# Normalising x four tiles at a time and moving the preparation of the unit conditions behind block 0's convolution

## The reference

```
shift, scale, gate = jnp.split(sc @ mod_w[i] + mod_b[i], 3, axis=-1)
cshift, cscale, cgate = jnp.split(scc @ mod_w[i] + mod_b[i], 3, axis=-1)
h_lat = rms_norm(x, norm_g[i]) * (1.0 + scale[:, None]) + shift[:, None]
h_ctx = rms_norm(ctx, norm_g[i]) * (1.0 + cscale) + cshift
...
u_lat, g_lat = jnp.split(h_lat @ w_in, 2, axis=-1)
u_ctx, g_ctx = jnp.split(h_ctx @ w_in, 2, axis=-1)
xc_lat = dwconv(u_lat, conv_w, conv_b)
xc_ctx = dwconv(u_ctx, conv_w, conv_b)
```

## Time and profile before

| | |
|---|---|
| median of 3 runs | 2920.01 us (2918.03 to 2926.49) |
| the profiled execution | 2916.92 us, of which the span is 2915.2 us |
| PE busy | 2729.0 us, 94% of the span |
| DVE busy | 1832.3 us, 63% |
| ACT busy | 1212.9 us, 42% |
| DMA, mean over the span | 168 GB/s |

### The profile page before, as it was taken

One profiled execution on the slowest core, in us unless ns is written; L12 is line 12 of the kernel. 1 busy time (PEld: TensorE's weight loads), 2 busy tenths in 40 slices (PEclk: granted clock), 3 DMA queues, 4 the chain that ended last, 5 costly groups with the idle time before them and its releaser, 6 DMA issues.

```text
span 2915.2 us, 41872 instructions
## 1 busy us (share of the span) xinstructions
PE 2729.0 (94%) x14546; PEld 2196.1 (75%) x14546; DVE 1832.3 (63%) x2708; ACT 1212.9 (42%) x1859; POOL 314.7 (11%) x437
## 2 busy tenths in 40 slices
PE   5799999889899999999999899999998998999989
PEld 2477777678677777777778677888886776998879
DVE  4499999889646555465655522334545787774654
ACT  3256555522443434443444422323444224553643
POOL 1101001144000000000003100000000442110000
PEclk8799999999999999999999999999999997999999
DMA  8755545467355454454535454232221663883425
GB/s 361 293 169 184 163 158 169 144 218 232 145 180 195 160 187 173 173 182 179 186 116 185 150 190 148 93 99 88 73 72 44 208 207 123 285 279 110 129 91 168
DMA packets 118632, 488.90 MB, mean 168 GB/s; under 512 B 13584, under 2 KB 15632, under 8 KB 103440
## 3 DMA queue, kind: packets, MB, share of 16 engines
q1 hardware_dynamic: 74176, 267.49, 27.2%
q0 software_dynamic: 44368, 220.22, 21.9%
HBM read 485.56 MB, written 2.10 MB: 167 GB/s over the span
## 4 chain that ended last, share of the span: by engine, by line
PE 66%; DVE 18%; issue 8%; DMA 5%; ACT 2%; DVEq 1%; POOL 0%; ACTq 0%; POOLq 0%; SPq 0%
PE psum L247 17%; PE psum L249 17%; PE psum L248 17%; DVE w_lo L229 4%; DVE psum L334 4%; PE psum L261 3%; DMA y<-in_mod_weights 2%; DVE work L336 2%; DMA work<-in_mod_units 1%; PE psum L1459 1%; PE psum L935 1%; PE psum L978 1%; DVE work L820 1%; ACT w_hi L221 1%; PE psum L284 1%
## 5 line engine op out<-in xcount | busy, mean ns | idle before, releaser
L247 PE MATMUL psum<-h_hi,w_hi 128*128 128x512 f32 (+1 forms) x3808 | 1358.3, 357 | 60.0 <-DVE h_lo L461 34.0
L249 PE MATMUL psum<-h_hi,w_lo 128*128 128x512 f32 (+1 forms) x3808 | 1320.7, 347 | 0.0
L248 PE MATMUL psum<-h_lo,w_hi 128*128 128x512 f32 (+1 forms) x3808 | 1320.5, 347 | 0.0
L229 DVE TENSOR_TENSOR w_lo<-raw,w_hi 128x1024 fp32r<-128x1024 f32 x496 | 597.5, 1246 | 617.2 <-ACT w_hi L221 617.1
L247 PEld LDWEIGHTS psum<-h_hi,w_hi 128*128 128x128 f32 x3808 | 727.7, 191 | 181.0 <-DVE w_lo L229 38.5
L248 PEld LDWEIGHTS psum<-h_lo,w_hi 128*128 128x128 f32 x3808 | 729.1, 191 | 93.7 <-issue 10.0
L249 PEld LDWEIGHTS psum<-h_hi,w_lo 128*128 128x128 f32 x3808 | 727.9, 191 | 89.5
L221 ACT ACTIVATE w_hi<-raw 128x1024 fp32r<-128x1024 f32 x496 | 496.7, 1051 | 291.1 <-PE psum L249 276.7
L334 DVE SCALAR_TENSOR_TENSOR psum<-work,modraw 128x1024 f32<-128x1024 f32 x128 | 177.6, 1388 | 19.4 <-DMA work<-in_mod_units 19.2
L336 DVE SCALAR_TENSOR_TENSOR work<-work,modraw 128x1024 f32<-128x1024 f32 x128 | 162.1, 1266 | 0.0
L267 POOL DMA_DIRECT2D modraw<-in_mod_weights x80 | 42.6, 533 | 836.5 <-PE psum L261 826.9
(11 more groups left out here) (260 smaller groups left out, 2683.6 us busy)
## 6 DMA issues: line engine op xcount, KB each, us to landing
raw<-in_weights SPq DMA_DIRECT2D x496, 512.0 KB, 4.5
modraw<-in_mod_weights POOLq DMA_DIRECT2D x96, 1024.0 KB, 5.2
work<-in_mod_units POOLq DMA_DIRECT2D x128, 512.0 KB, 4.3
y<-in_mod_weights POOLq DMA_DIRECT2D x16, 1024.0 KB, 9.4
modraw<-in_mod_units POOLq DMA_DIRECT2D x32, 512.0 KB, 4.6
modraw<-in_cond_rows POOLq DMA_DIRECT2D x4, 1024.0 KB, 6.3
work<-in_gate_w POOLq DMA_DIRECT2D x16, 256.0 KB, 5.0
work<-in_x_t POOLq DMA_DIRECT2D x16, 256.0 KB, 3.6
```

What stands on the lines that cost most here:

```text
L229: dve.tensor_tensor(w_lo[:, par, half, :], raw[:, 2 * par + half, :], w_hi[:, par, half, :].bitcast(F32), ALU.subtract).then_inc(S["split_ ...
L247: pe.matmul(dst, hi, h_hi[:, k, 0:n], start=(k == 0), stop=False)
L248: pe.matmul(dst, hi, h_lo[:, k, 0:n], start=False, stop=False)
L249: mm = pe.matmul(dst, lo, h_hi[:, k, 0:n], start=False, stop=(k == KT - 1))
```

## The change

Four edits, and one that follows from them:

- The multiplication by the reciprocal root goes from two instructions over 16 tiles ahead of everything into `modulate(j)`, two instructions over four tiles each time. `mod_add(1)` thereby stands directly behind the reciprocal root on DVE.
- On ACT `mod_rows(1)` goes ahead of the four `split_hi` of the first two strips.
- On PE `mod_turn(1)` goes ahead of `products(2)`.
- `cb_tanh(0)` goes into block 0 on ACT, behind the high part of the next u strip; `cb_silu(0)` goes into block 0 on DVE, behind the convolution and the low part of the next u strip.
- ACT no longer waits for `h_ready` ahead of `cb_tanh(0)`; POOL's program is the same, and its wait for `cond_ready` 5 ahead of unit 0's loads remains.

```
@@ lru_act, block
                 next_strip(split_hi, act, su)
+                if isinstance(b, int) and b == 0:
+                    cb_tanh(act, 0)
                 act.wait_ge(S["strip_done"], sg.s + 1)
...
-            act.wait_ge(S["h_ready"], KT)
-            cb_tanh(act, 0)
             block(0, 0)
@@ lru_dve
             dve.wait_ge(S["pads_zero"], 1)
-            cb_silu(dve, 0)
...
                 next_strip(split_lo, dve, su)
+                if isinstance(b, int) and b == 0:
+                    cb_silu(dve, 0)
                 unit(dve, 2 * b, 0, GATE + b)
@@ start_act
             norm_sqrt(act, 0)
+            mod_rows(act, 1, first_bank[1])
             for c in range(2):
                 split_hi(act, 0, c)
...
-            mod_rows(act, 1, first_bank[1])
             high(0)
@@ start_dve
             dve.wait_ge(S["rstd_done"], 1)
-            for x, s in ((xl[:, :, :], 0), (y[:, 1, :, :], 1)):
-                dve.tensor_tensor(x, x, nb["rstd"][:, s * T:(s + 1) * T].unsqueeze(1).to_broadcast([P, KT, T]),
-                                  ALU.mult).then_inc(S["xn_done"], 1)
...
                 ks = bass.ds(4 * j, 4)
+                for s, x in enumerate((xl[:, ks, :], y[:, 1, ks, :])):
+                    dve.tensor_tensor(x, x, nb["rstd"][:, s * T:(s + 1) * T].unsqueeze(1).to_broadcast([P, 4, T]),
+                                      ALU.mult).then_inc(S["xn_done"], 1)
                 dve.wait_ge(S["mod_cols"], 2 * j + 2)
...
-                dve.wait_ge(S["xn_done"], 2)
+                dve.wait_ge(S["xn_done"], 2 * j + 2)
@@ start_pe
             norm_pe(pe, 0)
+            mod_turn(pe, 1, 0, first_bank[1])
             for j in range(1, MOD_FIRST // 2):
                 for par in range(2):
                     products(2 * j + par, par)
-                    mod_turn(pe, 2 * j + par - 1, 0, first_bank[1 - par])
+                    if j > 1 or par > 0:
+                        mod_turn(pe, 2 * j + par - 1, 0, first_bank[1 - par])
```

## The result

The changed kernel took 2928.94 us in the median of 7 runs (2926.09 to 2936.66), the kernel before 2918.93 us beside it (2909.28 to 2926.49). The ratio is 1.0044 with a 95% interval of 1.0026 to 1.0061, so 8 to 18 us slower. In a second series on another occasion the ratio was 1.0036 (1.0023 to 1.0049), in medians 2929.03 to 2917.00. The forecast was 2931 with a range of 2923 to 2937, from a sum of 12.1 us over the kernel before; the medians give 10.0 and 12.0, the ratios 12.8 and 10.5.

The account below looks back on a forecast made before the run. The prediction took transfers, with one hole, to bound the start and DVE to set the pace in the LRU blocks. Its terms, 2.5 us (start) + 9.6 us (block 0) = 12.1 us on a base of 2919, gave 2931 us, range 2923 to 2937.

Parts of the forecast that it names:

- The start bound by transfers: Start, from 18 us on: chunks of modulation weights set the pace, with one hole in the transfers around 50 to 56 us.
- the stall of 3.55 us: Start: PE stands until 61.76 us for DVE's mod_add(1); removing it was put at no gain, upper end 3.55 us.
- The turn ahead of the products delays the refill by 2.5 us: Start: group 3's first load issued 1.3 + 1.6 - 0.4 = 2.5 us later, carried whole to the start's end.
- The multiplication by parts is covered: Start, modulate on DVE: 2.35 us more per group; idle time covers groups 1 and 2, PE's margin group 3.
- the 0.8 us that I counted: End of start: tile 12 ready at 130.2 us, PE wanting it at 131.0; 0.8 us of cover.
- Block 0 costs 9.6 us: LRU block 0, DVE: silu 5.1 us plus 4.5 us standing still for unit 0's load, 9.6 in sum.
- DVE carries it to the end: LRU blocks to output stage: DVE has no idle time to swallow 9.6 us, so output starts later by all of it.
- DVE's delay is swallowed: Rival, LRU blocks: PE sets the pace, DVE has over 9.6 us to spare; only 2.5 us left, 2921.5; chance 0.08.
- PE's stall was real: Rival, start: the wait delayed the slots' refill, so 3.55 us come back; 6.1 us slower, 2925; chance 0.14.
- DVE's early work was the bound: Rival, start: it followed DVE's path, so 6.5 us come off and a further 5.1 with silu moved; 2908; chance 0.05.
- collisions on top: Rival: start loses 3.2 us, tile 12 late 2 us, unit 0's loads meet raw weights; 16.7 us, 2936; chance 0.15.
- A tanh 1.4 us later: Block 0, ACT: by the skill page's table-load drain, tanh ready 1.4 us later and the sum about 1.4 higher.

Follow-up runs that it names:

- Filling both holes: Kernel before plus multiplication by parts, group 1's rows ahead, group 2's products spread over the norm, first tiles one by one behind chunks: 2913.27 us against 2917.47, ratio 0.9985.
- the conditions alone: Kernel before with only tanh and silu of the conditions moved into block 0, start unchanged: 2925.18 us against 2917.00, ratio 1.0030.
- the parts alone: Kernel before with only the multiplication by parts, group 1's rows and turn left in place: 2919.83 us against 2917.50, ratio 1.0007.
- the start alone: Kernel before with multiplication by parts and group 1's rows and turn ahead, conditions as before: 2921.17 us against 2917.00, ratio 1.0011.

## Why the prediction was right

**The start bound by transfers, the stall of 3.55 us worth nothing.** Shown for the stall: taking it away alone changes nothing that can be measured, and PE waits for chunks instead. Filling both holes gains 4.2 us on the kernel before, so the holes cost; but PE's clock moves the same stretch by as much, so the transfers are not its only limit.

**The turn ahead of the products delays the refill by 2.5 us.** The load came 3.04 us later: 1.17 of waiting (1.3 in the sum), 1.87 of turn (1.6), and no credit for a clock that rises (0.4), since it stayed at the half. So this was the upper end, 3.2, rather than the value taken. The edit of the start then costs 3 to 5 us in the timed series, while at the end of the start the traces have 1 to 2. That the 3 us are carried one to one, as I wrote, is not shown: the same stretch differs by 5 us from one execution of the same kernel to the next.

**The multiplication by parts is covered.** True in the changed kernel, where its last `modulate` ended ahead of PE. I had not seen that with the conditions left ahead it takes their cover; the 0.8 us that I counted were PE's margin at tile 12, and the narrower one was DVE's at the convolution, 0.6 to 1.5 us.

**Block 0 costs 9.6 us.** It cost 9.01: the silu 4.77 (5.1 in the sum, with two small waits for the tanh that fell away) and the wait for unit 0's load 4.24 (4.5). The tanh was ready, as forecast.

**DVE carries it to the end.** The distance from the convolution to L531 shows it: 407.6 to 408.1 us before, 417.2 with the conditions alone. PE's wait for DVE at the first output product is in the timeline of the changed kernel:

```profile
561.13 0.77 PE L531 MATMUL psum<-h_hi,w_hi 128*128 128x512 f32 x1 [7.09 <-DVE h_lo L516]
```

It lasts 7.09 us as before, and in every kernel of the study, to 0.01 us; the output stage starts whenever DVE is ready. The 7.09 us are therefore no spare time of PE, as the prediction took them: had PE had a pace of its own in the blocks, the wait would have grown with DVE's 9 us. Here L531 stands at 561.1, where the three traces of the kernel before have 545.5, 547.2 and 548.6, 14 us later on the mean. From there to the end the kernels' traces take 2366 to 2373 us, in no order that goes with the edits (2366.0 to 2369.7 before, 2367.6 and 2367.8 changed).

**A term that the sum lacked.** From the convolution to L531 the changed kernel takes 11.7 us more, not 9. Another 2.2 us are waits of DVE for unit loads behind unit 0: 3.0 and 2.7 us in its two traces, 0.5 to 0.9 before. Up to the convolution it takes only 0.7 us more than the two like traces of the kernel before, where the sum had 2.5. In these traces the start's term came out smaller, a term that the sum lacked came in, and the two nearly cancel. So the close agreement of 12.1 with the time is in part luck: the 9 us of block 0 are shown, the split of the other 3 is not.

**The median.** Setting the base at 2919, between the profiled execution and the median, fitted: the longer series of the kernel before have medians of 2917.0 to 2918.9. Against 12.1 the medians have 10.0 in the first series and 12.0 in the second, the ratios 12.8 and 10.5; the differences are inside the noise.

**The rivals.** "DVE's delay is swallowed" falls with the conditions alone. "PE's stall was real" falls with the parts alone; its 6.1 us had left out the 2.5 us of the turn, with which it would have been 8.6 and hard to tell from the forecast by the time. "DVE's early work was the bound" falls with the start alone, which is not faster. Of "collisions on top", the half clock was there, but in the kernel before too. No load took long at unit 0; the waits came at later units. A tanh 1.4 us later, as the prediction weighs it, would have added some 0.3 us and not 1.4, since the first had 1.1 us to spare (141.4 against 142.48).

**What would show it.** The bias of group 7 came at 128.87, not near 126.2, and the strip's copy at 140.75, not 139.2; both were set from the one lucky trace. Group 3's first load came at 55.72, with L416 2.1 us earlier in this trace; counted from L416 it is 57.8 on the old time, near the 57.3. "No DVE wait from there to the output stage" was wrong by the 3.0 us for unit loads, and L531 came 14 us later than the mean before, not 12. The other marks came as listed.

## What to carry to other kernels

Work that an engine does while it waits for something else is free only there: before moving it, look at how busy the engine is at its new place, and at every transfer that waits for its end. A stall in front of a buffer that is refilled by transfers is worth something only if the data had landed; the wait of the next chunk tells. And where the clock or the phase of a queue differs between executions, a second and a third trace of the same kernel come before any explanation of a few microseconds.

## What the runs showed of the hardware

The same start took 85.1 us in one execution and 90.4 in two others, with the granted clock from 70 to 82 us at 1.00 (2.4 GHz throughout) in the first and at a mean of 0.75 in the second. Counted from L416, the first execution has 1.00 from 14 to 32 us; the second has it from 14 to 16 and then 0.50 (1.2 GHz) from 18 to 26. Where they part, PE is at the end of group 3's products in both. The program is the same, so no edit made the 5 us.

A table load on ACT was followed by the next instruction after 1.29 us (143.26 to 144.55), as in the earlier trace rows. The Trainium skill (ScalarE: Activation LUTs, What ACT_TABLE_LOAD costs) has a drain of 1.38 us more for each switch; this case's traces show none, neither behind the load nor ahead of it (the instruction ahead ended at 143.24). The Trainium skill's rule to issue a DMA early and wait for it late (DMA: Bandwidth & Descriptors, Rules for kernel authors) is what the edit in block 0 went against, for 4.24 us.

In the blocks behind, DVE waited for unit loads 3.0 us in the changed kernel (five times) and 2.7 in its second trace, against 0.9, 0.5 and 0.6 in the traces of the kernel before:

```profile
DVE psum L334 <- DMA work<-in_mod_units: 3.0, 5, 1.0
```

The loads are the same. The longest from issue to landing between 186 and 545 us took 6.0 us in the changed kernel and 5.3 in the first trace before. That some of them fall onto a weight strip's transfer, depending on how DVE stands to PE after block 0, is a guess that no run tests.
